# Two norms between two transformer halves folded into the next layer's input

## The reference

```python
def rms_norm(x, g):
    y = x * lax.rsqrt(jnp.mean(x * x, axis=-1, keepdims=True) + EPS)
    return y * g
...
    # first block, last line
    return rms_norm(h, final_norm)
...
    # second block, its first layer
    h = rmsnorm(x, e_norm_mix[e])
    x = x + even_mixer(h, e_w_in[e], ...)
```

## Time and profile before

| | us |
|---|---|
| median of 3 runs | 2529.38 |
| lowest, highest | 2527.14, 2529.92 |
| the profiled execution, its own time | 2531.64 |
| its span | 2529.8 |
| PE busy | 2370.3 |
| DVE busy | 1318.5 |
| ACT busy | 957.7 |
| POOL busy | 280.9 |

### The profile page before, as it was taken

The page is one execution under the profiler, slowest core; times in us unless marked ns, Lnnn a source line. Parts: engine busy times, 40 slices in busy tenths (PEclk is TensorE's granted clock), DMA queues, the critical chain, the costliest instruction groups (busy, mean ns, idle before and its releaser), DMA issues.

```text
span 2529.8 us, 30118 instructions
## 1 busy us (share of the span) xinstructions
PE 2370.3 (94%) x11732; PEld 1867.3 (74%) x11732; DVE 1318.5 (52%) x1529; ACT 957.7 (38%) x1392; POOL 280.9 (11%) x188
## 2 busy tenths in 40 slices
PE   7999999999998989999998999999996689999997
PEld 6775667888876667888886678888875547788886
DVE  6447656664545656664647653333365565443333
ACT  3327753442322543442423533232225353332221
POOL 0000003110112003110100032110040001311010
PEclk9999999999999999999998999999998789999998
DMA  4211002222222002222232022322221101222231
GB/s 174 100 67 34 2 18 83 100 99 86 97 98 94 34 34 85 98 99 100 83 110 99 34 83 90 110 91 92 100 86 56 50 1 67 84 100 98 87 114 67
DMA packets 31202, 202.53 MB, mean 80 GB/s; under 512 B 4356, under 2 KB 5256, under 8 KB 7432
## 3 DMA queue, kind: packets, MB, share of 16 engines
q1 hardware_dynamic: 29816, 198.14, 22.2%
q10 hardware_dynamic: 1296, 3.15, 0.3%
HBM read 199.17 MB, written 2.10 MB: 80 GB/s over the span
## 4 chain that ended last, share of the span: by engine, by line
PE 83%; DVE 11%; ACT 4%; issue 1%; DMA 0%; ACTq 0%; DVEq 0%; SPq 0%
PE D L526 71%; PE X L600 3%; PE D L621 2%; PE D L613 2%; DVE neg_max L1680 2%; DVE w_lo L1475 1%; DVE xg L1509 1%; ACT prob L1177 1%; PE X L605 1%; ACT w_hi L1003 1%; DVE mid L1475 1%; DVE prob L1695 1%; ACT mid L1003 1%; PE X L717 1%; PE X L566 1%
## 5 line engine op out<-in xcount | busy, mean ns | idle before, releaser
L526 PE MATMUL D<-xg,w_hi 128*128 128x512 f32 x3184 | 1000.3, 396 | 57.1 <-DVE xg L1509 33.7
L526 PEld LDWEIGHTS D<-xg,w_hi 128*128 128x128 f32 x3184 | 604.4, 191 | 191.0 <-DVE w_lo L1475 25.7
L526 PE MATMUL D<-mid,w_hi 128*128 128x512 f32 x2312 | 719.2, 392 | 15.8 <-DVE w_lo L1475 7.7
L1475 DVE TENSOR_TENSOR w_lo<-w_raw,w_hi 128x2048 fp32r<-128x2048 f32 (+1 forms) x208 | 454.2, 2185 | 375.2 <-ACT w_hi L1003 374.9
L526 PE MATMUL D<-xg,w_lo 128*128 128x512 f32 x1592 | 626.3, 393 | 0.0
L1003 ACT ACTIVATE w_hi<-w_raw 128x2048 fp32r<-128x2048 f32 (+1 forms) x208 | 356.5, 1714 | 476.5 <-PE D L526 474.7
L526 PEld LDWEIGHTS D<-mid,w_hi 128*128 128x128 f32 x2312 | 436.3, 189 | 112.8 <-issue 17.6
L526 PE MATMUL D<-mid,w_lo 128*128 128x512 f32 x1156 | 452.2, 391 | 0.0
L526 PEld LDWEIGHTS D<-xg,w_lo 128*128 128x128 f32 x1592 | 303.3, 190 | 64.1
L526 PEld LDWEIGHTS D<-mid,w_lo 128*128 128x128 f32 x1156 | 218.7, 189 | 45.9
L1524 DVE TENSOR_TENSOR h<-D,h 128x1024 f32 (+1 forms) x72 | 88.0, 1222 | 267.8 <-PE D L526 267.8
(11 more groups left out here) (241 smaller groups left out, 1711.6 us busy)
## 6 DMA issues: line engine op xcount, KB each, us to landing
w_raw<-in_weights SPq DMA_DIRECT2D x184, 1024.0 KB, 4.8
h<-in_x SPq DMA_DIRECT2D x4, 512.0 KB, 7.9
out_y<-h SPq DMA_DIRECT2D x4, 512.0 KB, 2.7
inv_cnt<-in_inv_cnt ACTq DMA_DIRECT2D x1, 1024.0 KB, 4.9
cos<-in_cos ACTq DMA_DIRECT2D x3, 256.0 KB, 4.9
sin<-in_sin ACTq DMA_DIRECT2D x3, 256.0 KB, 5.3
vec<-in_vec SPq DMA_DIRECT2D x1, 262.0 KB, 3.0
cos<-in_cos_m ACTq DMA_DIRECT2D x1, 256.0 KB, 2.9
```

Source lines behind the costliest of these rows:

```text
L526: last = nc.tensor.matmul(out, w[a], x[b], start=start and k == 0, stop=stop and k == 2)
L1475: return nc.vector.tensor_tensor(out, x, f(high), ALU.subtract)
```

## The change

"between" leaves the list of layers. With r the root of the first norm, f and e the two gains and D the number of channels, the even layer's normalised input is h·f·e divided by the root of mean((h·f)²) + EPS·(mean(h²) + EPS). So:

- The two gains are multiplied once, early (`fold`), and `xg` of the even layer is h times that product. It is now made in the last phase of the second ffn, from h as the residual leaves it.
- POOL sums h² in that phase, as for other layers; ACT squares h·f into `sq_all`, two instructions per step, and DVE adds those up (`sum_block_squares`).
- `norm_sums` of the even layer makes both sums, DVE joins them, ACT takes two roots, DVE two reciprocals, and PE spreads both, into X[:, 2] and X[:, 1]. ACT copies the first to `rstd_b` and the second to `sq`.
- h itself, the residual, is multiplied by f and `sq` by DVE inside the even layer, between the pool evictions and the rotary (`scale_block`).
- The even layer's own norm no longer needs squares by ACT and sums by DVE at the start of that layer.

```diff
-LAYERS = ("nsa", "ffn", "swa", "ffn", "between", "even", "mlp", "odd", "mlp")
+LAYERS = ("nsa", "ffn", "swa", "ffn", "even", "mlp", "odd", "mlp")
...
+        def two_norms(norm):
+
+            return 0 < norm < L_END and layers[norm] == "even"
+
+        for l in range(L_END):
+            if two_norms(l):
+                GAIN[l] = VEC["fold"]
+
         def wide_norm(norm):
 
-            return norm in (0, L_END) or layers[norm] == "between" or layers[norm - 1] == "between"
+            return norm in (0, L_END)
...
                 for t in range(QT):
                     last = nc.tensor.matmul(X[:, 3, t:t + 1], ssum[:, span(t)], ones_col[:, :],
                                             start=True, stop=True)
+                if two_norms(norm):
+                    pe.wait_ge(block_summed, 1)
+                    for t in range(QT):
+                        last = nc.tensor.matmul(X[:, 3, QT + t:QT + t + 1], sq_all[:, 0, span(t)], ones_col[:, :],
+                                                start=True, stop=True)
                 last.then_inc(ms_done, 1)
                 pe.wait_ge(rstd_done, norm + 1)
...
+                if two_norms(norm):
+                    for t in range(QT):
+                        last = nc.tensor.matmul(X[:, 1, span(t)], block_rstd[:, t:t + 1].to_broadcast([P, P]),
+                                                ident[:, :], start=True, stop=True)
                 last.then_inc(rstd_x, 1)
...
+                if two_norms(norm):
+                    act.wait_ge(two_ready, 1)
+                    rms(two_rms[:, 0:QT], two_sums[:, 0:QT], DM)
+                    nc.scalar.activation(two_rms[:, QT:], two_sums[:, QT:], ACT.Sqrt, scale=1.0 / DM,
+                                         bias=vec[:, VEC["eps2"]:VEC["eps2"] + 1]).then_inc(rms_done, 1)
...
                 copy(rstd_b[:, :], X[:, 2, :]).then_inc(rstd_in, 1)
+                if two_norms(norm):
+                    copy(sq[:, :], X[:, 1, :]).then_inc(block_in, 1)
...
                         act.wait_ge(d_free[(u0 + n) % 2], (u0 + n) // 2 + 1)
                         gain_high(l + 1, n)
+                        if two_norms(l + 1):
+                            for k in (2 * n, 2 * n + 1):
+                                c = VEC["final1"] + k
+                                ins = nc.scalar.activation(sq_all[:, k, :], h[:, k, :], ACT.Square,
+                                                           scale=vec[:, c:c + 1])
+                            ins.then_inc(block_squared, 1)
...
+                if two_norms(norm):
+                    dve.wait_ge(ms_done, norm + 1)
+                    nc.vector.tensor_copy(two_sums[:, 0:QT], X[:, 3, 0:QT])
+                    link(nc.vector.tensor_copy(two_sums[:, QT:], X[:, 3, QT:2 * QT]))
+                    nc.vector.scalar_tensor_tensor(two_sums[:, QT:], two_sums[:, 0:QT], EPS, two_sums[:, QT:],
+                                                   ALU.mult, ALU.add).then_inc(two_ready, 1)
+                    dve.wait_ge(rms_done, norm + 1)
+                    nc.vector.reciprocal(block_rstd[:, :], two_rms[:, 0:QT])
+                    nc.vector.reciprocal(rstd_t[:, :], two_rms[:, QT:]).then_inc(rstd_done, 1)
+                    return
...
+            def sum_block_squares(t):
+
+                dve.wait_ge(block_squared, t + 1)
+                if t == 0:
+                    return
+                link(nc.vector.tensor_tensor(sq_all[:, 0:2, :], sq_all[:, 0:2, :], sq_all[:, 2 * t:2 * t + 2, :], ALU.add))
+                if t == 3:
+                    nc.vector.tensor_tensor(sq_all[:, 0, :], sq_all[:, 0, :], sq_all[:, 1, :],
+                                            ALU.add).then_inc(block_summed, 1)
...
                 for n in range(4):
                     if n + ahead <= 4:
                         split_low(u0 + n + ahead)
+                    if two_norms(l + 1) and n:
+                        sum_block_squares(n - 1)
                     if wide_norm(l + 1) and n:
                         sum_squares(l + 1, n - 1)
                     residual(u0 + n, n)
-                    if l + 1 < L_END and layers[l + 1] != "between":
+                    if l + 1 < L_END:
                         gain_low(l + 1, n)
...
+            def scale_block(l):
+
+                dve.wait_ge(block_in, 1)
+                for k in range(KD):
+                    c = VEC["final1"] + k
+                    nc.vector.scalar_tensor_tensor(h[:, k, :], h[:, k, :], vec[:, c:c + 1], sq[:, :], ALU.mult, ALU.mult)
...
                 ins.then_inc(d_free[u % 2], 1)
+                if two_norms(l):
+                    scale_block(l)
                 query_rotary("even", l, 0, 0)
...
+                nc.vector.tensor_tensor(vec[:, VEC["fold"]:VEC["fold"] + 8], vec[:, VEC["final1"]:VEC["final1"] + 8],
+                                        vec[:, VEC["e_norm"]:VEC["e_norm"] + 8], ALU.mult)
```

More of the change, by code:

```diff
@@ L118, in vector_columns @@
         ("lru_ba", 8), ("lru_bx", 8), ("lru_lam", 8),
[L119 removed]
+        ("ffn_w0", 132), ("ffn_b0", 44), ("ffn_w1", 132), ("ffn_b1", 44), ("cmp_pos", 32), ("eps", 1), ("eps2", 1), ("fold", 8),
     ):
@@ L200, in build_program @@
         sq = sb("sq", [P, SEQ])
+        two_sums = sb("two_sums", [P, 2 * QT])
+        two_rms = sb("two_rms", [P, 2 * QT])
+        block_rstd = sb("block_rstd", [P, QT])
         neg_max = sb("neg_max", [P, 4])
@@ L307, in build_program @@
         ms_done = sem("ms_done")
+        block_squared = sem("block_squared")
+        block_summed = sem("block_summed")
+        two_ready = sem("two_ready")
+        block_in = sem("block_in")
         rms_done = sem("rms_done")
@@ L394, in build_program @@
         N_CONST = 15
-        splits_before = totals(layers, {kind: 1 for kind in PHASES if kind != "between"})
+        splits_before = totals(layers, {kind: 1 for kind in PHASES})
         inner_before = totals(layers, {"ffn": FFN_TILES, "mlp": MLP_TILES // 2})
@@ L986, in odd @@
                 out_product(l, at)
-            programs = {"between": between, "nsa": nsa, "swa": swa, "even": even, "odd": odd}
+            programs = {"nsa": nsa, "swa": swa, "even": even, "odd": odd}
             for l, kind in enumerate(layers):
@@ L1044, in rstd_copy @@
             def rstd_copy(norm):
-                act.wait_ge(ms_done, norm + 1)
-                rms(rms_t[:, :], X[:, 3, 0:QT], DM).then_inc(rms_done, 1)
-                if norm == L_END or layers[norm] == "between":
+                if two_norms(norm):
[3 more added lines that the diff above has]
+                                         bias=vec[:, VEC["eps2"]:VEC["eps2"] + 1]).then_inc(rms_done, 1)
+                else:
+                    act.wait_ge(ms_done, norm + 1)
+                    rms(rms_t[:, :], X[:, 3, 0:QT], DM).then_inc(rms_done, 1)
+                if norm == L_END:
                     return
@@ L1070, in last_phase @@
                         square(n)
[L1072 to L1078, removed]
             def ffn_unit(l, u, f, slot, tile, i=0):
@@ L1547, in last_phase @@
                     sum_squares(l + 1, 3)
+                if two_norms(l + 1):
+                    sum_block_squares(3)
             def scale_h(l, t):
@@ L2115, in _ @@
                 at = first[l]
-                if kind == "between":
-                    continue
                 if kind in INNER:
@@ L2272, in pack_vectors @@
     out[:, VEC["eps"]] = EPS
+    out[:, VEC["eps2"]] = EPS * EPS
     pos = x["a_cmp_pos"][0].reshape(2, 2, 8, P).transpose(0, 2, 1, 3)
```

5 lines of the change are left out of this document (removed).

## The result

| | before | change |
|---|---|---|
| median, us (7 runs each) | 2529.38 | 2538.58 |
| lowest, highest | 2527.14, 2531.88 | 2537.6, 2540.3 |
| ratio, 95% interval | | 1.0037 [1.0025, 1.0048] |
| span of the profiled execution | 2529.8 | 2538.5 |

A forecast was written before the change was run, and what follows sets the result against it. PE bounds the kernel (83% of the chain), so only idle between the two halves counts: that stretch falls from 56.3 to 49.9 us, 6.4 less, taking the median from 2529.38 to 2523.0, range 2519.0 to 2527.0.

The forecast's parts named there:

- Both kernels do the same until 1310.2: Before the second ffn's last-phase residuals: no difference assumed; only the 56.3 us from there to 1366.52 was rebuilt.
- C: Second ffn's last phase: DVE and POOL lock each other out in every two-input instruction; 3.5 us slower, 2532.9; chance 0.04.
- zero: 1310.2 in the kernel before: end of unit 0 of the second ffn's last phase, where DVE's residual starts.
- the 30 matmuls: Even layer's first products after PE stops for xg's fourth quarter at 36.0: 8.74 us, ending at 44.7.
- small norm chain: Even layer, after the 30 matmuls: 2.51 us plus 2.7 added for second sums, root, reciprocal and spreading; PE back at 49.9.
- The new step: Second ffn's last phase: DVE sets the pace, w_lo takes 3.37 not 2.29; PE waits 1.0, 1.0 and 2.2 us.
- even sharing: Alternative price for w_lo beside POOL: a shared port costs about 0.6, ending at R+8.7 rather than R+9.2.
- Rival B: Clock falls again after the norm chain (2.6 us) or scaling outgrows its slack; saving 2.5 to 4.4, 2525 to 2527; chance 0.20.
- rival A: w_lo loses less (0.5 per step) or the clock holds at 7.14 (1.6); saving 8 to 9.5, 2520 to 2521.4; chance 0.17.
- Covered work: POOL and DVE sums at least 4 us under the 30 matmuls; h's scaling with 1.0 us to spare; cost 0.
- Rival D: PE arrives earlier but waits for the next thing, such as q_last's w_lo; nothing gained, 2529; chance 0.04.

The follow-up runs named there:

- experiment 9: The change with mid at its old place (experiment 2), plus DVE's block sum moved behind the residual, into its wait for ACT: 2516.57 us, ratio to kernel before 0.9954.
- experiment 2: The change with mid at its old place: small new tiles allocated last, gain product written over the first layer's gain columns; 2520.35 us, ratio to kernel before 0.9969.
- experiments 1: The kernel before with 128 unused bytes per partition in front of mid, nothing else changed: 2543.49 us against 2528.5, ratio 1.0064.
- experiment 8: The kernel before with 128 unused bytes between xg and the raw weights, so weights and mid move and xg stays: 2545.15 us, ratio 1.0067.
- experiment 7: The kernel before with 128 unused bytes in front of h, its first large tile, so everything moves together: 2526.73 us, ratio 0.9998.

## Why the prediction was wrong, step by step

**The step that failed** is the last but one sentence of the first part and what stands silently behind the sum: "Both kernels do the same until 1310.2, and this is the stretch I rebuild." They run the same instructions until then, except for the product of the gains, but not in the same time. I costed every instruction that the change adds and none of the tiles that it adds. The missing term is 3468 matmuls on `mid` at 5.5 ns each, +19.1 us of PE's time (1190.5 against 1171.4), of which 18.2 to 18.7 us came through to the time (2538.58 against 2520.35 and 2519.9). 2520.35 lies in the forecast range, 2538.58 11.6 us above its upper end. None of my four rivals held this; the one with the right sign, C, had its price at another place. So the mechanism that was forecast (work leaves a place where PE stands still, and the place gets shorter) was right, and a term that the sum put at nothing without a word outweighed it.

**The rebuilt stretch held, with one term mis-sized.** Counted from zero, forecast and measured in the changed kernel:

| | forecast | change | change, mid at old place |
|---|---|---|---|
| starts of the residuals apart | 9.2, 10.45, 10.45 | 9.06, 10.35, 10.30 | 9.07, 10.34, 10.30 |
| the 30 matmuls begin at | 36.0 | 35.6 | 35.6 |
| they take | 8.74 | 8.72 | 7.14 |
| small norm chain | 5.2 | 6.8 | 6.8 |
| PE back at | 49.9 | 51.1 | 49.6 |
| saved of 56.3 | 6.4 | 5.2 | 6.7 |

- *The new step.* Right to 0.2 us: `w_lo` took 3.38 where POOL runs beside it, as the earlier trace rows had it (3.37), and 2.28 in its last call of the phase, when POOL was all but done (its last sum ends at 1352.55). The rule that the two exclude each other for whole instructions (the Trainium skill, "SBUF — State Buffer", who interferes with whom) held again; even sharing would have ended `w_lo` 0.5 us earlier. PE's waits were smaller than forecast, 2.9 us in all for `w_lo` against 4.2 and 2.7 for `xg`'s last quarter against 3.0, but PE had to wait for that quarter in any case, so the 30 matmuls begin where DVE's work lets them (35.6 against 36.0).
- *The norm chain.* Here 1.6 us are missing in the forecast. The added DVE and ACT instructions cost what I took; the two spreadings took 2.08 and 1.71 us where I had counted 1.16 each, the price of the earlier trace rows (1.16 and 0.89 in experiment 9, at clock 1.00). A window of the changed kernel shows the granted clock at 0.56:

```profile
1359.50:1364.50 5.00, 3.75 (x17) 3.75 (x18) 0.61 (x5) 0.49 (x2) 0.52 (x1) 0.56 0.00 0
```

  Rival B named a clock that falls with the longer chain, and put the fall behind it. It fell in both places. The 120 matmuls behind the chain took 27.24 us before; in the change, and in the change with `mid` at its old place:

```profile
1364.53 28.43 PE D L538 x120
```

```profile
1358.13 28.30 PE D L538 x120
```

  The first 2.5 us of them ran at clock 0.51 in the change. So 1.1 to 1.2 us of the saving in the table are given back behind its last row, where B had feared 2.6. In experiment 9, where the chain ran at clock 1.00 in 4.97 us, they take 27.24 again. A duration read at one clock is a price at that clock.
- *The 30 matmuls.* 8.72 in the profiled execution of the change (granted clock 0.72 over the first 1.95 us, 0.83 over the next 6.7), 7.14 at clock 1.00 in that of experiment 2. Both of the forms of the earlier trace rows occur here too, and rival A's part came true in one kernel and not in the other.
- *What was luck.* In experiment 2 the stretch gave 6.7 where 6.4 was forecast, but two misses of the clock cancel in it: the chain 1.6 us dearer, the 30 matmuls 1.6 us cheaper.
- *Covered work.* All of it was covered. The scaling of h ended at 1413.04 and DVE then still waited 0.82 us for PE's swap, where 1.0 us of slack was forecast. POOL's last sum ended 5.2 us ahead of the chain:

```profile
1350.36 2.19 POOL L2150 TENSOR_SCALAR ssum<-ssum 128x512 f32<-128x512 f32 x1 [0.25 <-POOL ssum L2135]
```

- *Rival D.* The `w_lo` of q_last is in the chain of the changed kernel too, from 1402.63, but it moved with PE, as argued; nothing was given back there.
- *The size without the fault.* 8.2 us (interval 5 to 11) against 6.4. The stretch accounts for 6.7, less the 1.1 given back behind it. The remaining 2.6 is within the interval and I don't assign it; the two profiled executions reach zero 1.7 us apart (1308.58 against 1310.24), ahead of all that the change moves.

## What to carry to other kernels

Cost what a change allocates as well as what it executes: compare the start bytes of all matmul operands before and after, and where a phase gets slower in busy time and not in waits, look at the mean ns of its instructions by tile first. Here one line of unused bytes turned a change that loses 9 us into one that gains 8. And where one engine's sequence sets a step, look for a known wait in it before adding work ahead of it: moving DVE's 1.2 us sum into its 1.4 us wait for ACT made the stretch 5.0 us shorter in the trace, 2.9 by the steps themselves and most of the rest by the clock.

## What the runs showed of the hardware

- A matmul of 128*128 by 128x512 in this fp32r kernel takes about 5 ns longer when the streamed tile lies 128 or 192 bytes off a multiple of 256 from the weights' tile in the partition, and 1.4 ns longer at 64 bytes off. Offsets of 128 and 192 bytes cost 17 us of PE's busy time over 3468 such matmuls (1188.4 and 1187.9 against 1171.4), 64 bytes about 5 (1176.2), 256 bytes nothing (1169.6). Moving the streamed tile or moving the weights has the same effect (experiments 1 and 8), and moving both together has none (experiment 7). It shows with no other engine and no DMA at work (48 matmuls in 10.91 against 10.67 us). The granted clock wasn't the reason: over the whole execution it was 0.976 in the change, and 0.976 with `mid` at its old place.
- Why the distance counts isn't settled. In the trace the weight load of the next matmul runs beside the stream of the current one, so a meeting of the two reads in some part of SBUF would fit; no run tested that, nor whether other widths or types show it, nor what an offset under 64 bytes does. The Trainium skill ("TensorE: Matmul & The Clock Gate", step-by-step: what each phase is for) says that loading the next weights takes no read bandwidth from the running matmul, since PE has two independent read ports. By that the distance between the two operands could cost nothing; experiment 8, where `xg` became 16 us slower by a move of the weights alone, speaks against it for these fp32r matmuls.
- The clock after short stops differs between profiled executions by as much as a term of this forecast: the 30 matmuls behind the stop took 7.14 us in experiment 2 and 8.72 in the change, which has the same instructions. Within one kernel, experiment 2, the mean granted clock was 0.976 in an execution of 2517.74 us and 0.972 in one of 2523.57.
